# Block sums T2, T3, T4 of the normalised rows by VectorE from kept f32 rows in place of identity products on TensorE

## The reference

```python
y = jnp.concatenate([mix, mo], axis=-1) @ w_out[i]
x = layer_norm(DN_ALPHA * x + y, ln_mix_g[i], ln_mix_b[i])
f = (jax.nn.silu(x @ w_gate[i]) * (x @ w_up[i])) @ w_down[i]
x = layer_norm(DN_ALPHA * x + f, ln_ffn_g[i], ln_ffn_b[i])
```

## Time and profile before

| | us |
|---|---|
| median of three runs | 2209.46 |
| the three runs | 2209.74, 2209.46, 2207.75 |
| the profiled execution | 2207.05 |
| its span, first to last instruction | 2205.3 |

### The profile page before, as it was taken

The page is one execution under the profiler, slowest core; times in us unless marked ns, Lnnn a source line. Parts: engine busy times, 40 slices in busy tenths (PEclk is TensorE's granted clock), DMA queues, the critical chain, the costliest instruction groups (busy, mean ns, idle before and its releaser), DMA issues.

```text
span 2205.3 us, 32142 instructions
## 1 busy us (share of the span) xinstructions
PE 2167.9 (98%) x11056; PEld 1842.6 (84%) x11056; DVE 1299.6 (59%) x2419; ACT 927.9 (42%) x1747; POOL 1300.0 (59%) x847
## 2 busy tenths in 40 slices
PE   8999999999999999999999999999999999999997
PEld 7888888878888888888888899988888888888885
DVE  5555565666545655665547746657535555555567
ACT  5655555622434444333324653213443333343323
POOL 4321222373678777777773793424768777777773
PEclk9999999999999999999999999999999999999999
DMA  5221212141012111111131312201011111111122
GB/s 178 63 57 45 58 48 58 44 136 57 20 39 67 58 49 53 50 57 48 57 96 52 107 35 58 77 20 58 20 58 58 58 57 57 57 57 53 52 61 83
DMA packets 164444, 133.16 MB, mean 60 GB/s; under 512 B 12144, under 2 KB 147952, under 8 KB 164336
## 3 DMA queue, kind: packets, MB, share of 16 engines
q1 hardware_dynamic: 148992, 115.36, 17.3%
q10 hardware_dynamic: 15344, 16.35, 2.6%
HBM read 122.78 MB, written 4.19 MB: 58 GB/s over the span
## 4 chain that ended last, share of the span: by engine, by line
PE 93%; DVE 3%; POOL 1%; ACT 1%; DMA 1%; issue 1%; ACTq 0%; DVEq 0%; POOLq 0%
PE ps L338 27%; PE ps L340 27%; PE ps L339 27%; PE ps L691 3%; PE ps L719 1%; PE ps L720 1%; PE ps L678 1%; PE ps L679 1%; PE ps L1512 1%; PE ps L1104 1%; POOL Rl L1816 1%; PE ps L1017 1%; DVE V L2304 1%; DMA raw<-in_w_gate 0%; PE ps L729 0%
## 5 line engine op out<-in xcount | busy, mean ns | idle before, releaser
L2013 DVE TENSOR_TENSOR XR<-XR,ps 128x512 f32<-128x512 f32 x504 | 339.0, 686 | 214.7 <-PE ps L340 214.7
L311 POOL TENSOR_TENSOR Wh<-raw,zcol 128x1024 fp32r<-128x1024 f32 x76 | 144.5, 1902 | 465.8 <-PE ps L340 394.0
L1816 POOL TENSOR_TENSOR Rl<-raw,Rh 128x512 fp32r<-128x512 f32 x216 | 278.9, 1292 | 138.9 <-ACT Rh L1660 136.4
L338 PE MATMUL ps<-XTh,Wh 128*128 128x512 f32 x608 | 248.7, 409 | 1.4 <-DVE XTl L1033 0.7
L340 PE MATMUL ps<-XTh,Wl 128*128 128x512 f32 x608 | 238.3, 392 | 0.0
L339 PE MATMUL ps<-XTl,Wh 128*128 128x512 f32 x608 | 237.7, 391 | 0.0
L340 PE MATMUL ps<-XTh,Rl 128*128 128x512 f32 x576 | 224.1, 389 | 0.0
L338 PE MATMUL ps<-XTh,Rh 128*128 128x512 f32 x576 | 224.1, 389 | 0.0
L339 PE MATMUL ps<-XTl,Rh 128*128 128x512 f32 x576 | 224.1, 389 | 0.0
L1660 ACT ACTIVATE Rh<-raw 128x512 fp32r<-128x512 f32 x216 | 135.8, 630 | 156.2 <-PE ps L340 146.3
L338 PE MATMUL ps<-Wh,XTh 128*128 128x256 f32 (+1 forms) x576 | 191.8, 333 | 1.0 <-DVE mixL L966 0.7
(11 more groups left out here) (307 smaller groups left out, 5586.0 us busy)
## 6 DMA issues: line engine op xcount, KB each, us to landing
raw<-in_w_gate SPq DMA_DIRECT2D x44, 512.0 KB, 3.7
raw<-in_w_up SPq DMA_DIRECT2D x44, 512.0 KB, 3.8
rows<-in_w_down SPq DMA_DIRECT2D x36, 512.0 KB, 3.6
raw<-in_a_w_in SPq DMA_DIRECT2D x20, 512.0 KB, 3.7
raw<-in_w_out SPq DMA_DIRECT2D x16, 512.0 KB, 3.5
raw<-in_b_w_in SPq DMA_DIRECT2D x15, 512.0 KB, 3.8
B<-in_c_bias SPq DMA_DIRECT2D x12, 512.0 KB, 3.5
raw<-in_w_mem_kv SPq DMA_DIRECT2D x8, 512.0 KB, 4.0
```

Of the source, the lines that this page charges most:

```text
L311: nc.gpsimd.tensor_tensor(high, raw[:, turn, :], zcol[:, 0:1].to_broadcast([P, UNIT]), ALU.add).then_inc(high_done, 1)
L338: nc.tensor.matmul(dst, wh, xh, start=first, stop=False, skip_group_check=onto)
L1816: nc.gpsimd.tensor_tensor(Rl[(w - 1) % 4][:, :], source(w), Rh[(w - 1) % 4][:, :].bitcast(F32), ALU.subtract).then_inc(gs[L]("low"), 1)
L2013: nc.vector.tensor_tensor(x, x, bank(4 + i), ALU.add).then_inc(gf[L]("added"), 1)
```

## The change

- ScalarE's f32 rows are kept: each of the 16 units j gets a buffer of its own, `XF[j]`, in place of the three `fbuf` buffers, and the wait for the buffer goes. XF 0 to 3 hold block 11, 4 to 7 block 21, 8 to 11 block 12, 12 to 15 block 22. Some of them lie where weights, `S1` and the rings `Rh`, `Rl` come later.
- VectorE makes 12 f32 block sums of 128 x 512 from them, in place, SBUF to SBUF (`t_raw_dve`): T3 and T2 behind the low part of half i = 1, T4 behind the last addition of the first down products.
- The high and low parts of T2, T3 and T4 come from these buffers in place of PSUM banks. T2's are made behind half i = 2, on ScalarE and VectorE, T3's one behind each row tile t = 0 to 3, T1's behind t = 4 to 7, T4's at the end.
- TensorE keeps only T1: 4 jobs of 4 products, one behind each row tile 0 to 3. Its wait for T4 stands ahead of product 6. The signs are written behind the high part of half i = 2.
- GpSimd's weight sums wait for T3's raw sums, two of the eight shifts come ahead of the low parts of weights 4 and 3; the high parts of these wait for T3's last low part. SyncE's `row` loads wait for the last low part of all block sums.

```diff
@@ row_act @@
-        if j >= 3:
+        if j >= 3 and g not in go:
             act.wait_ge(*g("xt_low", j - 2))
...
-    T_JOBS = [(3, 2, 0), (3, 3, 1), (3, 0, 2), (3, 1, 3), (2, 2, 0), (2, 3, 1), (2, 0, 2), (2, 1, 3),
-              (4, 2, 0), (4, 3, 1), (1, 2, 0), (1, 3, 1), (1, 0, 0), (1, 1, 1), (4, 0, 2), (4, 1, 3)]
+    T1_JOBS = (2, 3, 0, 1)
+    T_ORDER = ([(2, k) for k in range(4)] + [(3, k) for k in range(4)] + [(1, k) for k in T1_JOBS]
+               + [(4, k) for k in (2, 3, 0, 1)])
+    T_RAW = [(n, k) for n in (3, 2, 4) for k in range(4)]
...
+    def t_pe(pe, L, b):
+
+        k = T1_JOBS[b]
+        if b == 0:
+            pe.wait_ge(*gs[L]("t_high", 2))
+        pe.wait_ge(*gf[L]("gated", 3 + b // 2 + 2))
+        ops = [(sign, block_of(x, q)(k)) for sign, q in ((plus, 12), (minus, 11)) for x in (XTh, XTl)]
...
     def t_after(pe, L):
         def after(t):
-            t_pe(pe, L, 2 * t)
-            t_pe(pe, L, 2 * t + 1)
+            if t < 4:
+                t_pe(pe, L, t)
...
+    def t_raw_dve(dve, L, n, k):
+
+        g = gs[L]
+        if n == 3:
+            dve.wait_ge(*go[L]("affine", 2 * KT))
+            dve.wait_ge(*go[L]("xt_low", 2 * KT))
+            dst, x, y, op = XF[12 + k], XF[12 + k], XF[8 + k], ALU.subtract
+        elif n == 2:
+            dve.wait_ge(*g("t_raw", t_raw(3, k)))
+            dst, x, y, op = XF[k], XF[12 + k], XF[k], ALU.add
+        else:
+            dve.wait_ge(*g("t_raw", t_raw(2, k)))
+            dst, x, y, op = XF[4 + k], XF[4 + k], XF[k], ALU.subtract
+        nc.vector.tensor_tensor(dst[:, :], x[:, :], y[:, :], op).then_inc(g("t_raw"), 1)
...
+        nc.scalar.activation(right(n)(k)[0], t_source(n, k), ACT.Copy).then_inc(g("t_high"), 1)
...
+        nc.vector.tensor_tensor(low, t_source(n, k), high.bitcast(F32), ALU.subtract).then_inc(gs[L]("t_low"), 1)
...
         if first:
             pe.wait_ge(*gf[L]("added", EARLY + gf[L].credit))
+            pe.wait_ge(*g("t_low", len(T_ORDER)))
             mul_prod(pe, L, apart(j), 6, 4, start=True)
...
+        elif first and w < 5:
+            act.wait_ge(*g("t_low", t_done(3, 3)))
...
-            sp.wait_ge(*g("t_made", 16))
+            sp.wait_ge(*g("t_low", len(T_ORDER)))
...
+            pool.wait_ge(*gs[L]("t_raw", t_raw(3, 3)))
             mul_sums_pool(pool, L, 0)
+            shifts_pool(pool, L, range(2))
             low_pool(pool, L, 0, 4)
             low_pool(pool, L, 0, 3)
-            shifts_pool(pool, L)
+            shifts_pool(pool, L, range(2, NT))
             pair_pool(pool, L, 0, first=True)
...
+            def sums_act(i):
+
+                if i != 2:
+                    return
+                act.wait_ge(*go[L]("xt_low", 2 * KT))
+                nc.scalar.activation(plus[:, :], ident[:, :], ACT.Copy).then_inc(gs[L]("t_high"), 1)
+                nc.scalar.activation(minus[:, :], ident[:, :], ACT.Copy, scale=-1.0).then_inc(gs[L]("t_high"), 1)
+                for k in range(4):
+                    t_act(act, L, 2, k)
...
-            for j in range(16):
-                t_act(act, L, j)
-                if j in (0, 1, 3):
-                    high_act(act, L, 0, {0: 2, 1: 4, 3: 3}[j], first=True)
+            for j in range(4, len(T_ORDER)):
+                t_act(act, L, *T_ORDER[j])
+                if j == 5:
+                    high_act(act, L, 0, 2, first=True)
+                if j == 7:
+                    high_act(act, L, 0, 4, first=True)
+                    high_act(act, L, 0, 3, first=True)
             pair_act(act, L, 0, first=True)
...
+            def sums_dve(i):
+
+                if i == 1:
+                    for n in (3, 2):
+                        for k in range(4):
+                            t_raw_dve(dve, L, n, k)
+                if i == 2:
+                    for k in range(4):
+                        t_dve(dve, L, 2, k)
+
...
                 acc_dve(dve, gf[L], 0, t, ALPHA)
-                for j in (2 * t, 2 * t + 1):
-                    t_dve(dve, L, j)
+                t_dve(dve, L, *T_ORDER[4 + t])
+            for k in range(4):
+                t_raw_dve(dve, L, 4, k)
+            for n, k in T_ORDER[12:]:
+                t_dve(dve, L, n, k)
             pair_dve(dve, L, 0, first=True)
```

More of the change, by code:

```diff
@@ L1119, in row_read, with row_f32 @@
         return g("odd_high" if j % 2 else "even_high", j // 2 + 1)
+    def row_f32(g, j):
+        return XF[j][:, :] if g in go else fbuf[:, j % 3, :]
     def row_act(act, g, j):
@@ L1142, in row_dve @@
         dve.wait_ge(*row_read(g, j))
-        nc.vector.tensor_tensor(xt_unit(XTl, j), fbuf[:, j % 3, :], xt_unit(XTh, j).bitcast(F32),
+        nc.vector.tensor_tensor(xt_unit(XTl, j), row_f32(g, j), xt_unit(XTh, j).bitcast(F32),
                                 ALU.subtract).then_inc(g("xt_low"), 1)
@@ L1272, in gains_pool, with shifts_pool @@
             nc.gpsimd.tensor_tensor(XR[:, t, :], XR[:, t, :], gb[:, 0, :], ALU.mult).then_inc(g("gained"), 1)
-    def shifts_pool(pool, L):
+    def shifts_pool(pool, L, tiles):
         pool.wait_ge(*go[L]("gb_scaled", 1))
-        for t in range(NT):
+        for t in tiles:
             pool.wait_ge(*gf[L]("added", 2 * t + 2 + gf[L].credit))
@@ L1495, in right @@
         return lambda k: (high(k), low(k))
[L1497 to L1510, removed]
+    def t_pe(pe, L, b):
[4 more added lines that the diff above has]
+        ops = [(sign, block_of(x, q)(k)) for sign, q in ((plus, 12), (minus, 11)) for x in (XTh, XTl)]
         for i, (sign, x) in enumerate(ops):
-            mm = nc.tensor.matmul(bank(b), sign[:, :], x, start=n in (1, 3) and i == 0, stop=i == len(ops) - 1,
-                                  skip_group_check=n in (2, 4))
+            mm = nc.tensor.matmul(bank(b), sign[:, :], x, start=i == 0, stop=i == len(ops) - 1)
         mm.then_inc(gs[L]("t_made"), 1)
@@ L1517, in after, with t_source, t_act, t_dve @@
         def after(t):
-            t_pe(pe, L, 2 * t)
-            t_pe(pe, L, 2 * t + 1)
-        return after
[L1522 to L1528, removed]
-        high, low = right(n)(k)
[L1530 to L1535, removed]
+            if t < 4:
+                t_pe(pe, L, t)
+        return after
+    def t_raw_dve(dve, L, n, k):
[11 more added lines that the diff above has]
+        nc.vector.tensor_tensor(dst[:, :], x[:, :], y[:, :], op).then_inc(g("t_raw"), 1)
+    def t_source(n, k):
+        return bank(T1_JOBS.index(k)) if n == 1 else XF[{2: 0, 3: 12, 4: 4}[n] + k][:, :]
+    def t_act(act, L, n, k):
+        g = gs[L]
+        if n == 1:
+            act.wait_ge(*g("t_made", T1_JOBS.index(k) + 1))
+        else:
+            act.wait_ge(*g("t_raw", t_raw(n, k)))
+        if n == 2:
+            act.wait_ge(*gf[L]("up", 3))
+        if n == 3:
+            act.wait_ge(*gf[L]("up", 4))
+        if n == 4 and k < 2:
+            act.wait_ge(*gf[L]("product", EARLY))
+        nc.scalar.activation(right(n)(k)[0], t_source(n, k), ACT.Copy).then_inc(g("t_high"), 1)
+    def t_dve(dve, L, n, k):
+        high, low = right(n)(k)
+        dve.wait_ge(*gs[L]("t_high", 2 + t_done(n, k)))
+        nc.vector.tensor_tensor(low, t_source(n, k), high.bitcast(F32), ALU.subtract).then_inc(gs[L]("t_low"), 1)
     def keep_act(act, L, m, j):
@@ L1617, in tile_pe @@
         mul_prod(pe, L, 0, 3, 2)
-        pe.wait_ge(*(g("t_low", 16) if first and not j else g("comb", 3 * s)))
+        pe.wait_ge(*(g("t_low", t_done(1, T1_JOBS[3])) if first and not j else g("comb", 3 * s)))
         mul_prod(pe, L, 2, 4, 1, start=True)
@@ L2080, in pair_last_dve, with ffn_first @@
         join_dve(dve, L, 0, 0)
-    def ffn_first(row, one, two):
+    def ffn_first(row, one, two, then):
         for j in range(KT, 2 * KT):
@@ L2093, in ffn_first @@
             two(i)
+            then(i)
     gvp, gup, gsg = Names("vproj"), Names("uproj"), Names("sgu")
```

23 lines of the change are left out of this document (14 added, 9 removed).

## The result

| | before | after |
|---|---|---|
| median us, measured side by side | 2208.97 | 2222.91 |
| lowest to highest of after's four runs | | 2222.41 to 2223.13 |
| span of the profiled execution | 2205.3 | 2221.4 |
| mean granted clock | 0.998 | 0.992 |

The kernel before has four runs here, the three of its own table and one more, so its median is 2208.97 and not 2209.46. The change makes the kernel slower: ratio 1.0066 [1.0054, 1.0077], +13.9 us. The forecast was +18.0 (2227.5), its range 2212 to 2233.

The account below looks back on a forecast made before the run. TensorE, busy 98%, was taken as the bound. Per layer -7.25 + 2.7 + 1.3 + 9.6 = +6.4 us, with the clock +9.0; two layers +18.0, from 2209.46 to 2227.5 us, range 2212 to 2233.

Parts of the forecast that it names:

- Removed matmuls: On TensorE, 32 identity products a layer go, 0.227 us each: 7.25 us a layer, 14.5 in all.
- The port: VectorE's operations with two SBUF inputs take turns with GpSimd's queued 1024-wide operations: one every 2.8 us.
- First stall: Before the first T1 product, TensorE waits for the signs, written late behind gating 2: 2.7 us a layer.
- Second stall: In the down units, TensorE waits to reuse a bank until the late first addition is done: 1.3 us a layer.
- Third stall: Before product 3, TensorE waits for ScalarE's copy of product 1, queued behind T4's late high parts: 9.6 us a layer.
- The clock: TensorE's clock falls to 1.2 GHz in the gap before product 3: 2.6 us a layer, bounds 0 to 3.2.
- What hides: Low parts of weights 5 to 7, the next tile's first low part and the moved row loads: no cost.
- (a): Rival: the port costs nothing, 0.6 us a sum; -6.4 us a layer, 2196.8 us; chance 0.11.
- (b): Rival: as forecast, but TensorE's clock stays up; +12.8 us, 2222.3 us; chance 0.16.
- (c): Rival: VectorE waits at the port but GpSimd isn't held; +3.2 us a layer, 2215.9 us; chance 0.10.
- (d): Rival: each turn holds GpSimd 0.6 us, clock costs 3.2; +11.3 us a layer, 2232.1 us; chance 0.08.

Follow-up runs that it names:

- signs run: Changed kernel with plus and minus written behind the high part of half 1 instead of half 2: 2223.25 us, ratio 1.007.
- the reordered ones: Kernels with the change and queues reordered, among them act_order (2224.49 us), order_sp (2213.18) and new order (2208.88).
- the kernel with the cut: Changed kernel with GpSimd's gain multiplies and shift additions cut from 1024 columns to 1: 2194.83 us, ratio 0.994.
- new order: Changed kernel with ScalarE and SyncE queue edits, early signs, gains after T3's and T2's raw sums, shifts rearranged: 2208.88 us, ratio 1.0001.
- act_order: Changed kernel with ScalarE's four T4 high parts moved behind the copies of products 1 and 3: 2224.49 us, ratio 1.0073.
- early: Changed kernel with GpSimd's first four gain multiplies of a layer moved ahead of the last normalised units: 2221.61 us, ratio 1.0058.
- b_early: Kernel before the change with GpSimd's first four gain multiplies of a layer moved ahead of the last normalised units: 2216.83 us, ratio 1.0036.
- order_sp: act_order with SyncE's next weight-half loads put ahead of its wait for T4's last low part and the row loads: 2213.18 us, ratio 1.0022.

## Why the prediction was right, by its own steps

- **Removed matmuls.** 32 x 0.227 = 7.25 a layer. Right: 64 fewer on the page (10992 against 11056), and with the stalls gone 12.8 us came back.
- **The port, 2.8 us a sum.** Right: eight in 21.39, 2.67 each, median 2.876; the eight gains 22.02 in place of 19.7 (578.47 to 598.21). The 19.7 already hold two held multiplies, and the first of the 22.02 is free. The seven behind it, from 580.67 to the weight sum at 600.30, lie 2.80 apart, 0.45 above the free 2.35; I had 0.43 from one pair of rows.
- **First stall 2.7.** Right: 2.63, at the sign, as named. Not foreseen was what follows it: the clock fell after this gap too and cost 1.6. I had asked only of the 9.6 whether the clock falls; behind the 2.7 its price was put at nothing without a reason.
- **Second stall 1.3.** Absent, but not wrong as a chain: TensorE came later by the low clock's 1.6, and the addition was there. The signs run, with no fall of the clock there (granted 1.00 from 600 to 612), shows it with 1.5. The two terms exchange: 1.3 forecast, 1.6 paid. That they are nearly equal is luck; I had foreseen the one and not the other.
- **Third stall 9.6.** The mechanism right, the size 8.29: T4's sums ended at 640.3 in place of 641.1, and TensorE was ready for product 3 at 634.3 (642.62 - 8.29) in place of 633.8. The 0.8 is a wait of GpSimd's that did not come: T3's last low part ended at 619.6 and not at 621.8, so the low parts of weights 4 and 3 followed shift 1 at once, at 621.82, and shifts 2 to 7 began at 624.32 in place of 625.1. The 0.5 is product 1's later start, 628.72 against 628.3, with rounding.
- **The clock 2.6.** Right that it falls, 1.9 in place of 2.6. The price came from 128-column transposes at the start, in which DMA arrivals were mixed.
- **What hides.** The next tile's first low part ended at 656.2 (forecast 655.4), TensorE came at 658.06 (657.0), and no wait stood there. The row loads' move cost nothing in the changed kernel, and that is all it was tested for there. In the reordered ones it cost first by its place in the queue (5.18 us), then perhaps by the traffic.
- **Rivals.** (a), port free: shown false for this kernel; the kernel with the cut, where the port costs next to nothing, came near its price, 2194.83 against my 2196.8. (b), clock stays: false. (c), GpSimd not held: its time, 2215.9, was not met, and GpSimd's 22.02 against 19.7 speaks against it. (d): false.

The sum, -7.25 + 2.7 + 1.3 + 9.6 + 2.6 = 9.0 a layer, against -7.25 + 2.63 + 1.6 + 8.29 + 1.9 = 7.2: the 1.8 lie in the third stall (1.3) and the clock behind it (0.7), less 0.3 by which the unforeseen fall of the clock outweighs the second stall.

The Trainium skill, "SBUF — State Buffer", section "Who interferes with whom", was named as a rule against the change, and the traces agree: VectorE's sums of two SBUF inputs take a median of 2.876 us beside GpSimd's long operations and 0.684 without them.

## What to carry to other kernels

Before work is moved from TensorE to VectorE, look at what GpSimd does in the same microseconds: an operation of 0.69 us with two SBUF inputs costs 2.8 when GpSimd has 1024-column operations queued, and a share of 59% busy says nothing about it. Idle time of GpSimd is no room either if VectorE has such operations there. In a kernel whose main engine has no slack, a stall that is taken away uncovers the next in line (here ScalarE's queue, SyncE's queue, GpSimd's load, a transfer), so ask of each thing costed at nothing what it costs once its cover is gone.

## What was unexpected of the hardware

- The clock fell after a wait of 2.63 us that came between stretches of full work: four matmuls after the gap ran 0.23 to 0.34 apart, the eight after them 0.427, and 605 to 612 us had 0.76 granted. In the new order a wait of 2.73 did the same (starts 0.42 apart from 649.95 on, 0.66 granted from 650 to 655). But the same wait for the sign, 2.61 us, left the clock up in layer 0 of act_order:

```profile
605.00:612.00 7.00, 6.23 (x28) 4.76 (x27) 6.22 (x10) 5.06 (x11) 1.87 (x2) 1.00 0.16 1
```

- Other pairs say the same. A wait of 2.50 us near 575 us left the clock at 1.00 in early and lowered it (0.66 from 575 to 580) in b_early. In act_order a wait of 2.27 in layer 0 left it up and one of 1.84 in layer 1, at 1629.25, did not. Waits of 1.6 and 1.5 in the signs run left it up. So these runs do not let the fall be told from the length of a wait of 1.8 to 2.7 us; behind the waits of 5.2 us and more in the runs told of here it always came, as the forecast had it for the third stall. What lay between the fall and the return was eight or nine 512-column matmuls in most cases, 1.6 to 1.9 us lost, after 8.29 us of idling hardly more than after 2.63; the extremes seen were six matmuls (order_sp, at 604.63) and twelve (act_order, at 1644.85).
- The Trainium skill, "TensorE: Matmul & The Clock Gate", section "What's actually happening", calls the low clock the default that activity releases. The traces agree in so far as the low clock stood behind the waits of 5.18 and 8.29 us, and the matmuls that followed brought the high one back.
- The turns at the port held in both places where VectorE and GpSimd had full queues of such operations: four T2 low parts beside the late gains took 11.30 us in the new order, 2.8 each, and the eight raw sums of the changed kernel 21.39, 2.67 each (the last of them stood beside a shorter operation, a weight sum).
